# Stick-breaking heads: the mask leaves TensorE; the scan takes a maximum with ones in the masked half, and GpSimd zeroes masked sigmoids

## The reference, cut to what matters

```python
def sb_attend(q, k, v, q_pos, k_pos):
    z = jnp.einsum("bqhd,bkhd->bhqk", q, k, preferred_element_type=jnp.float32) * (HEAD_DIM ** -0.5)
    mask = k_pos[None, :] < q_pos[:, None]
    log_1m = jnp.where(mask, jax.nn.log_sigmoid(-z), 0.0)
    suffix = lax.cumsum(log_1m, axis=3, reverse=True) - log_1m
    a = jnp.where(mask, jnp.exp(jax.nn.log_sigmoid(z) + suffix), 0.0)
    return jnp.einsum("bhqk,bkhd->bqhd", a.astype(v.dtype), v)
```

## Time and profile before

| | |
|---|---|
| median of three runs | 1066.63 us |
| the profiled execution | 1068.08 us |
| its span, first to last instruction | 1066.3 us |
| TensorE busy | 95% of the span |
| VectorE, ScalarE, GpSimd busy | 62%, 43%, 24% |
| granted TensorE clock, mean | 0.994 of full speed |

### The profile page before, as it was taken

How to read it: one execution, slowest core, us unless ns; L and a number is a source line. 1 busy time by engine, 2 the same in 40 slices (tenths; PEclk the granted TensorE clock), 3 DMA queues, 4 the chain that set the end, 5 groups by cost and what they waited for, 6 DMA issues and landing times.

```text
span 1066.3 us, 27354 instructions
## 1 busy us (share of the span) xinstructions
PE 1017.2 (95%) x11316; PEld 858.2 (80%) x11316; DVE 661.0 (62%) x979; ACT 463.4 (43%) x911; POOL 257.4 (24%) x198
## 2 busy tenths in 40 slices
PE   6899999999999999999999998999988999999997
PEld 5898778986778888888878987777766788887886
DVE  5557455654565546565645723676767877787487
ACT  5522312222021232232222323676687787787353
POOL 2300000000000010111201110400065566667596
PEclk9999999999999999999999999999998999999999
DMA  6366787798889787779878787855444452421343
GB/s 228 109 242 230 241 325 290 259 362 317 306 319 353 289 312 284 300 261 369 318 297 299 267 250 232 232 137 130 111 94 93 96 110 60 98 70 51 138 164 133
DMA packets 121328, 234.02 MB, mean 219 GB/s; under 512 B 60536, under 2 KB 91256, under 8 KB 103808
## 3 DMA queue, kind: packets, MB, share of 16 engines
q1 hardware_dynamic: 95872, 209.33, 58.1%
q10 hardware_dynamic: 25344, 23.08, 6.3%
HBM read 204.52 MB, written 27.86 MB: 218 GB/s over the span
## 4 chain that ended last, share of the span: by engine, by line
PE 80%; DVE 5%; issue 4%; ACT 4%; POOL 3%; DMA 2%; ACTq 1%; DVEq 0%; SPq 0%; POOLq 0%
PE bank L887 28%; PE bank L874 8%; PE bank L951 7%; PE bank L997 6%; PE bank L1246 6%; PE bank L1665 6%; PE bank L1222 5%; PE bank L1199 5%; PE bank L980 3%; DVE pr L1468 2%; PE bank L1261 1%; PE bank L1177 1%; DMA k_buf<-in_cache_sb_k 1%; PE bank L940 1%; POOL o_nat L1834 1%
## 5 line engine op out<-in xcount | busy, mean ns | idle before, releaser
L887 PE MATMUL bank<-w_hi,hT_hi 128*128 128x256 f32 (+1 forms) x896 | 260.7, 291 | 3.5 <-DVE hT_lo L620 3.1
L887 PE MATMUL bank<-w_lo,hT_hi 128*128 128x256 f32 (+1 forms) x896 | 253.2, 283 | 0.2 <-issue 0.2
L887 PE MATMUL bank<-w_hi,hT_lo 128*128 128x256 f32 (+1 forms) x896 | 252.9, 282 | 0.0
L887 PEld LDWEIGHTS bank<-w_hi,hT_hi 128*128 128x128 f32 x896 | 170.6, 190 | 11.1 <-issue 5.4
L887 PEld LDWEIGHTS bank<-w_lo,hT_hi 128*128 128x128 f32 x896 | 170.8, 191 | 0.5 <-issue 0.4
L887 PEld LDWEIGHTS bank<-w_hi,hT_lo 128*128 128x128 f32 x896 | 170.6, 190 | 0.0
L534 ACT ACTIVATE u_out<-bank 128x256 f32<-128x256 f32 x112 | 42.9, 383 | 273.7 <-PE bank L887 273.5
L730 DVE STREAM_TRANSPOSE k_buf<-k_buf 128x2048 f32<-128x2048 f32 x64 | 145.4, 2292 | 7.8 <-DMA k_buf<-in_cache_sb_k 7.0
L1478 DVE TENSOR_TENSOR_SCAN om<-om 128x1024 f32<-128x1024 f32 (+3 forms) x64 | 110.0, 1721 | 17.0 <-ACT om L1382 16.3
L1546 POOL TENSOR_TENSOR pr<-pr,om 128x1023 f32<-128x1023 f32 (+3 forms) x64 | 93.3, 1463 | 72.5 <-DVE om L1478 68.7
L1222 PE MATMUL bank<-ident,pr 128*128 128x128 f32 x576 | 87.8, 280 | 9.9 <-POOL pr L1546 4.6
(11 more groups left out here) (203 smaller groups left out, 1931.3 us busy)
## 6 DMA issues: line engine op xcount, KB each, us to landing
k_buf<-in_cache_fox_k SPq DMA_DIRECT2D x32, 1024.0 KB, 9.4
v_ring<-in_cache_fox_v SPq DMA_DIRECT2D x32, 1024.0 KB, 6.8
k_buf<-in_cache_sb_k SPq DMA_DIRECT2D x32, 1024.0 KB, 9.2
v_ring<-in_cache_sb_v SPq DMA_DIRECT2D x32, 1024.0 KB, 6.6
w_raw<-in_w_in SPq DMA_DIRECT2D x14, 1024.0 KB, 8.7
out<-u_out ACTq DMA_DIRECT2D x72, 128.0 KB, 5.3
q_scratch<-u_out ACTq DMA_DIRECT2D x64, 128.0 KB, 5.5
k_nat<-out SPq DMA_DIRECT2D x32, 256.0 KB, 3.9
```

The costliest lines, as they stand in the source:

```text
L887: mm = pe.matmul(bank[:, U + i % 2, w_cols(c)], a[:, k, hcols(s)], b[c % 2][:, k, w_cols(c)], start=(k == 0 and n == 0), stop=(k == KD - 1 ...
```

## The change

The stick-breaking heads no longer add the mask on TensorE. The scores of masked entries stay as computed, so both sigmoids there have ordinary values, and two things put them right. The scan has a new second operand, `hidden`, an int8 array with ones in the masked half of the last 128 columns and zeros elsewhere, and takes the maximum of the running product and this operand: in the masked half the product stays 1. And GpSimd zeroes the masked half of the last 128 columns of `pr` with an affine_select before it multiplies. `hidden` is made once, by four GpSimd instructions after `split_wo`, in the last 1024 bytes of the place of `c_b`, with `sa` as scratch. `mask[1]` is still built at the start but no longer used. FoX heads are as before.

```diff
+        hidden = place(AT_K + 12288 - SEQ, "hidden", [P, SEQ], I8)
+        pr_shown, hidden_made = sem("pr_shown"), sem("hidden_made")
@@ scores
-                    diagonal = seg == i // 4
+                    diagonal = seg == i // 4 and not g
                     if diagonal:
-                        mm = pe.matmul(out[:, w - P:w], identb[:], mask[g][:], start=False, stop=True,
+                        mm = pe.matmul(out[:, w - P:w], identb[:], mask[0][:], start=False, stop=True,
                                        skip_group_check=True)
@@ scans
-                dve.tensor_tensor_scan(x, x, x, 1.0, ALU.mult, ALU.bypass).then_inc(scan_done, 1)
+                if isinstance(k, int) and k == 64:
+                    dve.wait_ge(hidden_made, 4)
+                dve.tensor_tensor_scan(x, x, hidden[:, SEQ - n:SEQ][:, ::-1], 1.0, ALU.mult, ALU.max).then_inc(scan_done, 1)
@@ pool_prompt
             split_wo(pool)
+            pool.wait_ge(s_moved, NU * (NHEAD // 2 - 1) + 3)
+            pool.memset(hidden[:], 0).then_inc(hidden_made, 1)
+            pool.wait_ge(hidden_made, 1)
+            pool.memset(sa[:, 0:P], 0.0).then_inc(hidden_made, 1)
+            pool.wait_ge(hidden_made, 2)
+            pool.affine_select(out=sa[:, 0:P], in_=sa[:, 0:P], compare_op=ALU.is_ge, fill=1.0, base=-1,
+                               pattern=[[-1, P]], channel_multiplier=1).then_inc(hidden_made, 1)
+            pool.wait_ge(hidden_made, 3)
+            pool.tensor_copy(hidden[:, SEQ - P:SEQ], sa[:, 0:P]).then_inc(hidden_made, 1)
             for h in range(NHEAD // 2, NHEAD):
                 for u in range(NU):
                     n, k = (TP - u) * P, NU * h + u
+                    pool.wait_ge(s_moved, k + 1)
+                    x = pr[:, u % 4, n - P:n]
+                    pool.affine_select(out=x, in_=x, compare_op=ALU.is_ge, fill=0.0, base=-1,
+                                       pattern=[[-1, P]], channel_multiplier=1).then_inc(pr_shown, 1)
+                    pool.wait_ge(pr_shown, k - 63)
                     pool.wait_ge(scan_done, k - 63)
-                    pool.wait_ge(s_moved, k + 1)
                     x = pr[:, u % 4, 0:n - 1]
                     pool.tensor_tensor(x, x, om[:, u % 4, 1:n], ALU.mult).then_inc(pb_ready, 1)
```

More of the change, by code:

```diff
@@ L17 @@
 F32R = mybir.dt.float32r
+I8 = mybir.dt.int8
 BF16 = mybir.dt.bfloat16
```

## The result

The change makes the kernel slower, and by more than twice what was forecast: 1086.18 us (median of four runs, 1080.92 to 1092.23) against 1066.88, a ratio of 1.0168 with a 95% interval of 1.0139 to 1.0198. Forecast were 1075.3 us and at most 1084. The direction was right, and so was the pair of engines at fault. The loss lay where the second half of R2 put it and not where the forecast's walk did, and a part of its price, TensorE's clock, was in no sum.

A forecast was written before the change was run, and what follows sets the result against it. TensorE was taken as the bound by a hair, with VectorE's and GpSimd's port turns right behind. Six heads +7.8, first +0.2, last +0.7 made +8.7 us, median 1066.63 to 1075.3; range 1066 to 1084, 8 in 10.

The forecast's parts named there:

- second half of R2: At u6: its product loses the port to the 1024-wide scan; about +1.8 us a head, +11 or 1078; joined the forecast (0.67).
- the forecast's walk: Settled head followed turn by turn: selects make products lose turns, TensorE stands 0.65 us (u3), 1.25 (u4); head 24.1 us.
- by a hair: Settled heads: TensorE bounds, with the VectorE-GpSimd loop right behind; slack 0.48 us at u4, about 0.15 at u6.
- R2: Rival at u6: selects slip under scans, product wins (+1 to +2 us, 1068, chance 0.10) or loses (1078, in forecast's 0.67).
- The mask matmul: TensorE, each unit: dropping it saves 0.07 us, 0.56 a head, 4.5 in all, if TensorE stays the bound.
- The chain of turns: VectorE scans and GpSimd products alternate at the port, practically without a hole from 907.41 us until u6.
- The scan with a maximum: VectorE's scans: the maximum and second operand leave the price at 2.1 ns a column; upper end 3.1 ns.
- The set-up of `hidden`: GpSimd after `split_wo`: four instructions, 1 to 4 us, fit into its 11.14 us wait and cost nothing.
- Selects wait for the port: GpSimd beside scans: a select, 0.29 us alone, needs the port and waits until the running scan ends.
- The sum itself: All stick-breaking heads: six settled +7.8, first +0.2, last +0.7, together +8.7 us.
- First head, +0.2: First stick-breaking head: select u0 comes out of a scan 0.3 us late, less 0.5 us of masks; net +0.2 us.
- Last head, +0.7: Last head, GpSimd on the path: selects of u3 and u4, 0.3 to 0.44 us each, and u6's, less masks; +0.7 us.

The follow-up runs named there:

- filler run: Changed kernel plus ten unused 128x512 matmuls on TensorE between `a_turn` and u6's transposes, heads 10 to 14: median 1082.5 us, six heads 149.4 us.
- second trace: The changed kernel run once more, nothing altered, for another trace: six heads 156.5 us against 155.6 in the first trace.
- memset: Changed kernel with a 128x128 memset in place of each affine_select, so GpSimd writes without reading: 1070 us.

## Why the prediction was right or wrong

- **The bound, "by a hair".** Right, and the most useful reading. What decides is how far u6's product starts ahead of the 1024-wide scan: 0.48 us before (920.64 against 921.12), 0.39 without masks and selects (919.68 against 920.07), 0.33 with all selects but u6's (924.25 against 924.58), 0.01 with the selects alone, and 0.06 us behind it after. So the masks' removal used up 0.09, the other seven selects of the head about 0.06, and u6's select of 0.29 with its 0.08 us of wait the rest. R2 had this place and both its outcomes (921.1 against 921.12).
- **The mask matmul, 0.07 us each, 0.56 a head if TensorE stays the bound.** The price of the matmul stands, the condition isn't met. Without selects 0.1 us a head arrived, and with GpSimd's gate work gone as well about 0.2 (22.85 to 22.66). The chain of turns was not only a second loop behind TensorE, it was the bound together with it, at several points, and so was ScalarE's copy at u2.
- **The scan with a maximum, 2.1 ns a column.** Right: 1.75 us for 768 columns after (884.81), and 1944 ns in the group mean as before.
- **The set-up of `hidden`, hidden.** Right: four instructions, 793.36 to 795.4, some 2 us, and the first scan started at 802.20, let go by ScalarE's `om` and not by GpSimd.
- **Selects wait for the port.** Right: 1.48, 1.22 and 0.95 us under the scans of u3 to u5, 706 ns in the mean, and memsets don't. The trace agrees with the page SBUF — State Buffer of the Trainium skill (section Who interferes with whom), which names a GpSimd instruction that reads SBUF, not one that only writes it.
- **The walk: stands of 0.65 at u3 and 1.25 us at u4.** This is the step that failed. It let u1's product end at 908.0 and held scan u2 up for 0.5 us by that. In the run without u6's select, where heads are 23 us and no stand gives room, that product ended 0.25 us after VectorE's copy of u7 began (910.94 against 910.69), on the walk's clock at 907.46. The walk also put 0.15 us between a select and its product (it is 0.08) and 0.2 us for what a held-up select still needs after the scan (it is 0.09). So after scan u3 the product of u3 was 0.2 us ahead of scan u4 (889.77 against 889.97) and kept its turn; in the walk it came behind. No stand at u3 or u4 in a settled head, and so TensorE reached u6 early. The loss fell there, by R2's second half, which had the mechanism ("stands behind 2.1 us of scan") and a price of its own, +1.8 a head; that price was short by the masks' gain that didn't arrive, by 0.2 us of stand and by the clock.
- **Where the walk's turn was lost.** Once in the six heads after, in the first. u3's product started 0.05 us behind scan u4, and TensorE stood 0.75 us at u4 and not at all at u3, against 0.65 and 1.25 in the walk. In the other five the product was 0.03 to 0.21 us ahead. The walk had a real mechanism with the turn on the wrong side of a small distance.

```profile
839.28 2.29 POOL L1564 TENSOR_TENSOR pr<-pr,om 128x639 f32<-128x639 f32 x1
```

```profile
843.75 0.66 PE L1225 MATMUL bank<-ident,pr 128*128 128x128 f32 x4 [0.75 <-POOL pr L1564]
```

- **The clock.** In no term of the sum. A stand of 2.6 us in one piece brought the half clock in four of five heads, 1.4 us more in such a head: 6.2 us of the 18.1 by the filler run. With the measured stand and this, the head comes to 22.85 + 2.6 + 1.4 - 0.1 = 26.7.
- **The sum itself.** 24.1 us is 1.25 over 22.85, so six heads are +7.5 and not +7.8; that changes nothing here.
- **First head, +0.2.** Not settled. From the first stick-breaking scan to the first `a_product` are 26.5 us before, and 25.8 and 26.6 in the two traces after.
- **Last head, +0.7.** The place was right, the size not: +2.3. Selects of u3 (1.22 us) and u4 (0.77 us) stood under scans where 0.3 to 0.44 each were put in, and TensorE waited 0.51 us for u3 (nothing before) and 2.83 us for u4 (2.38 before), 1.0 us more. The clock took about as much again: it is at half speed for 6.8 us there (from 1001.53), before for 3.4 us (from 988.56). In the second trace, with the same two waits and 3.4 us at half clock, this head takes 25.9 us and not 27.0, which puts the longer half clock at 1.1 us.

GpSimd, then TensorE, in the last head after; it answers to the earlier trace rows.

```profile
995.91 1.22 POOL L1559 TENSOR_SCALAR_AFFINE_SELECT pr<-pr 128x128 f32<-128x128 f32 x1
997.21 1.32 POOL L1564 TENSOR_TENSOR pr<-pr,om 128x639 f32<-128x639 f32 x1
998.48 1.92 POOL L1771 TENSOR_TENSOR zb<-zb,o_nat 128x512 f32<-128x512 f32 x1
1000.35 0.77 POOL L1559 TENSOR_SCALAR_AFFINE_SELECT pr<-pr 128x128 f32<-128x128 f32 x1
```

```profile
1002.35 1.12 PE L1225 MATMUL bank<-ident,pr 128*128 128x128 f32 x4 [2.83 <-POOL pr L1564]
```

What stays open: why the clock didn't fall behind every stand. In the head of 25.65 us TensorE stood as long (about 925.47 to 928.06 us) and the granted clock stayed at 1.00 until the product; in the second trace it stayed at 1.00 behind two of six such stands, with the selects alone it fell behind all five. No run was made to tell what decides.

## What to carry to other kernels

Where two engines take turns at a resource, an instruction of 0.3 us can cost what stands in the queue, if a turn is lost by it; here the hold was a scan of 2.3 us. Look for the smallest distance between a start on one engine and the next long hold on the other, here 0.48 us, and treat that distance as the slack. Here there were several such distances of a few tenths of a us, and the walk named the wrong one: give each a price of its own. The repair is order before work: moving 1.3 us of other work behind the critical product gave back 14 of 18 us. And a stall of TensorE in one piece is to be priced with the clock's fall that can follow it, here 1.4 us on top of 2.6.

## What the runs showed of the hardware

- A scan with two SBUF operands on VectorE and a reading instruction on GpSimd exclude one another for the whole instruction: 128x128 affine_selects, 0.29 us alone, took 0.67 to 2.28 us when started under a scan (after, 25 cases); 128x128 memsets took 0.19 to 0.22 us in all 64 cases, 38 of them under a scan.
- The recorded start tells the winner of such a turn only to within some 0.02 us: u6's products recorded 0.03 to 0.05 us ahead of the scan kept their turn (memset and filler runs), those 0.01 us ahead lost it (selects alone).
- The second operation of the scan (a maximum instead of none) and an int8 second operand changed nothing: 1944 against 1944 ns in the mean of eight scans of 768 columns.
- TensorE's granted clock fell to 1.2 GHz for 3.4 us behind stands of 2.3 to 2.4 us of recorded idle time: after in four of five, 0.5 to 1.2 us into the work that followed; in the second trace in four of six; with the selects alone in five of five. It stayed at 2.4 GHz when the stand was filled with ten matmuls of 128x512.
- A GpSimd instruction that waits for the semaphore of the one before it starts 0.08 us after that one's end (affine_select to product); between `a_silu` and `a_gain` it is 0.14 us (895.50 + 1.28 to 896.92).
